# Rows of bounds for the gated-memory cells: by DMA through DRAM, or by TensorE and ScalarE

## What is computed

```python
b = jnp.cumsum(fc, axis=-1)
dlog = jnp.where(causal, b[..., :, None] - b[..., None, :] + ic[..., None, :], -jnp.inf)
inter = b + m[..., None]
m_t = jnp.maximum(inter, jnp.max(dlog, axis=-1))
w_in = jnp.exp(dlog - m_t[..., None])
s = jnp.einsum('bhtd,bhsd->bhts', qc, kc) * w_in
num = jnp.einsum('bhts,bhsd->bhtd', s, vc) + ...
den = jnp.sum(s, axis=-1) + ...
h = num / jnp.maximum(jnp.abs(den), jnp.exp(-m_t))[..., None]
```

## Time and profile before

| | us |
|---|---|
| runs of the kernel before | 3138.63, 3146.48, 3146.72 (median 3146.48) |
| the profiled execution's own time | 3142.69 |
| its span | 3140.9 |
| the cells stage, first spread to the end of the last product on DVE and the barrier | 1618.0 to 1735.4 |
| PE, DVE, ACT busy in 1618.0 to 1735.4 | 96.4, 78.3, 67.5 |
| DVE's first mask | 1624.77 |
| granted PE clock 0.50 (1.2 GHz) in the stage | 1639.4 to 1642.8, 1663.3 to 1666.7, 1711.2 to 1714.5, and from 1724.7 on |
| granted PE clock, mean of the whole | 0.978 |

### The profile page before, as it was taken

How to read it: one execution, slowest core, us unless ns; L and a number is a source line. 1 busy time by engine, 2 the same in 40 slices (tenths; PEclk the granted TensorE clock), 3 DMA queues, 4 the chain that set the end, 5 groups by cost and what they waited for, 6 DMA issues and landing times. The chain is left out here.

```text
span 3140.9 us, 37997 instructions
## 1 busy us (share of the span) xinstructions
PE 3025.9 (96%) x15290; PEld 2632.7 (84%) x15290; DVE 1923.5 (61%) x2891; ACT 1125.7 (36%) x1669; POOL 89.3 (3%) x72
## 2 busy tenths in 40 slices
PE   7989999999999999999998899999999999999998
PEld 5778888887788888899986499999999978788886
DVE  5755775856664878766646755543554365488674
ACT  4454422234453222343346123221222345343232
POOL 0031000000040000000000000000000000000000
PEclk9998999999998999999999899999999999999999
DMA  3110554521102655512110121121121210245432
GB/s 127 54 34 27 186 172 142 196 89 61 48 14 91 198 180 187 165 64 101 63 33 18 41 95 61 61 69 57 63 66 63 95 50 1 79 169 200 169 132 83
DMA packets 79546, 298.78 MB, mean 95 GB/s; under 512 B 8555, under 2 KB 12203, under 8 KB 78220
## 3 DMA queue, kind: packets, MB, share of 16 engines
q1 hardware_dynamic: 79372, 296.35, 28.0%
HBM read 287.93 MB, written 8.39 MB: 94 GB/s over the span
## 5 line engine op out<-in xcount | busy, mean ns | idle before, releaser
L122 PE MATMUL banks<-normed_hi,weights_hi 128*128 128x512 f32 (+2 forms) x2320 | 843.1, 363 | 0.8 <-DVE normed_lo L561 0.8
L123 PE MATMUL banks<-normed_lo,weights_hi 128*128 128x512 f32 (+2 forms) x2320 | 840.2, 362 | 0.0
L104 ACT ACTIVATE weights_hi<-weights_raw 128x1024 fp32r<-128x1024 f32 (+3 forms) x365 | 395.4, 1083 | 1221.4 <-PE banks L125 1178.3
L125 PE MATMUL banks<-normed_hi,weights_lo 128*128 128x512 f32 (+2 forms) x2320 | 737.8, 362 | 0.0
L110 DVE TENSOR_TENSOR weights_lo<-weights_raw,weights_hi 128x1024 fp32r<-128x1024 f32 (+3 forms) x365 | 463.0, 1269 | 145.4 <-ACT weights_hi L104 140.7
L123 PEld LDWEIGHTS banks<-normed_lo,weights_hi 128*128 128x128 f32 x2320 | 438.4, 189 | 41.2
L122 PEld LDWEIGHTS banks<-normed_hi,weights_hi 128*128 128x128 f32 x2320 | 437.0, 188 | 42.7 <-DVE normed_lo L561 1.2
L125 PEld LDWEIGHTS banks<-normed_hi,weights_lo 128*128 128x128 f32 x2320 | 429.6, 189 | 41.0
L122 PE MATMUL banks<-hidden_hi,weights_hi 128*128 128x512 f32 (+1 forms) x880 | 323.1, 367 | 0.1
L123 PE MATMUL banks<-hidden_lo,weights_hi 128*128 128x512 f32 (+1 forms) x880 | 323.0, 367 | 0.0
L125 PE MATMUL banks<-hidden_hi,weights_lo 128*128 128x512 f32 (+1 forms) x880 | 294.7, 367 | 0.0
(11 more groups left out here) (447 smaller groups left out, 4246.9 us busy)
## 6 DMA issues: line engine op xcount, KB each, us to landing
weights_raw<-in_w_up SPq DMA_DIRECT2D x176, 512.0 KB, 3.3
ada_tiles<-in_ada SPq DMA_DIRECT2D x96, 512.0 KB, 3.3
weights_raw<-in_w_down SPq DMA_DIRECT2D x64, 704.0 KB, 4.0
weights_raw<-in_w_in SPq DMA_DIRECT2D x67, 512.0 KB, 3.3
up_rows<-in_up_rows SPq DMA_DIRECT2D x44, 512.0 KB, 3.4
weights_raw<-in_w_out SPq DMA_DIRECT2D x32, 512.0 KB, 3.2
x_kept<-x SPq DMA_DIRECT2D x2, 3072.0 KB, 11.0
x<-x_kept SPq DMA_DIRECT2D x1, 3072.0 KB, 10.1
```

Source lines behind the costliest of these rows:

```text
L104: act.activation(self.hi[:, n % 2, 0:w], self.raw[:, n % 2, 0:w], ACT.Copy).then_inc(self.high_ready, 1)
L122: pe.matmul(out, self.hi[:, s, m], xh, start=k == 0, stop=False)
L123: pe.matmul(out, self.hi[:, s, m], xl, start=False, stop=False)
L125: mm = pe.matmul(out, self.lo[:, s, m], xh, start=False, stop=k == kt - 1)
```

## The change

The rows of bounds no longer go through PE, PSUM and ACT. SP stores M to a DRAM tensor once, when `gate_rows` is given, waits for it, and then loads one row of it to all 128 partitions for each run. The first two loads are issued before the last projection tile is evacuated. The others are issued one by one, when ACT and DVE are through with the buffer's last run. The buffers `bound_rows` now lie over M and the sums beside it, which are not read any more by then (hence the wait for `gate_cols`). DVE and ACT wait for the load of their run, each parity having its own semaphore. The spread on PE and the copies on ACT are gone, and with them the waits on them. The computation is the same.

```diff
+        self.bounds = Z.nc.dram_tensor("bounds", (64, TOK), F32).ap()
...
-        self.Mb = buf("bound_rows", [P, 2, TOK])
+        self.Mb = Z.buffer("bound_rows", [P, 2, TOK], 24 * TOK * ROW)
...
+    def bounds_in(self, n):
+        return self.Z.mix["bounds_odd" if n % 2 else "bounds_even"]
+
+    def bounds_there(self, eng, n):
+        eng.wait_ge(self.bounds_in(n), 16 * (n // 2 + 1))
+
     def sync(self, sp):
-        Z = self.Z
+        Z, on = self.Z, self.Z.mix
+
+        def spread(n):
+            h, d = self.RUNS[n]
+            if n >= 2:
+                sp.wait_ge(on["cell_decays"], 6 * (n - 1))
+                sp.wait_ge(on["cell_masked"], 6 * (n - 1))
+            sp.dma_start(self.Mb[:, n % 2], self.bounds[32 * d + h].partition_broadcast(P)).then_inc(self.bounds_in(n), 16)
+        sp.wait_ge(on["gate_rows"], 1)
+        sp.dma_start(self.bounds, self.gates.M).then_inc(on["bounds_kept"], 16)
+        sp.wait_ge(on["bounds_kept"], 16)
+        sp.wait_ge(on["gate_cols"], 1)
+        for n in range(2):
+            spread(n)
         sp.wait_ge(Z.evacuated, self.last + 1)
...
         sp.wait_ge(Z.mix["network_in"], 32)
+        for n in range(2, 8):
+            spread(n)
         sp.wait_ge(Z.mix["cell_scores"], 4 * self.PER_HEAD)
...
     def tensor(self, pe):
-        def spread(n):
-            h, d = self.RUNS[n]
-            if n:
-                pe.wait_ge(on["bounds_copied"], n)
-            else:
-                pe.wait_ge(on["gate_cols_copied"], 2)
-            sel = K["ident"][0:64, 32 * d + h:32 * d + h + 1].broadcast_to([64, P])
-            for seg, (a, w) in enumerate(SEGS):
-                mm = pe.matmul(Z.spread_ps[:, seg, 0:w], sel, self.gates.M[:, a:a + w], start=True, stop=True)
-            mm.then_inc(on["bounds_spread"], 1)
...
-                pe.wait_ge(on["bounds_copied"], 8)
+                pe.wait_ge(on["gate_cols_copied"], 2)
...
-        spread(0)
         pe.wait_ge(Z.evacuated, self.last + 1)
...
-                if m == 2 and n + 1 < 8:
-                    spread(n + 1)
                 pe.wait_ge(on["cell_weights"], 6 * n + m + 1)
...
     def scalar(self, act):
-        def copy_rows(n):
-            act.wait_ge(on["bounds_spread"], n + 1)
-            if n >= 2:
-                act.wait_ge(on["cell_weights"], 6 * (n - 1))
-            for seg, (a, w) in enumerate(SEGS):
-                last = act.activation(Mb[:, n % 2, a:a + w], Z.spread_ps[:, seg, 0:w], ACT.Copy)
-            last.then_inc(on["bounds_copied"], 1)
-            act.wait_ge(on["bounds_copied"], n + 1)
...
-        copy_rows(0)
...
+                if m == 0:
+                    self.bounds_there(act, n)
...
-                if m == 3 and n + 1 < 8:
-                    copy_rows(n + 1)
...
         def mask(q):
-            dve.wait_ge(on["bounds_copied"], n + 1)
+            self.bounds_there(dve, n)
```

More of the change, by code:

```diff
@@ L2494 @@
 class Cells(Stage):
-    COUNTS = ["v_cells_turned", "v_cells_copied", "bounds_spread", "bounds_copied", "cell_scores", "cell_scores_copied",
+    COUNTS = ["v_cells_turned", "v_cells_copied", "bounds_kept", "bounds_even", "bounds_odd", "cell_scores", "cell_scores_copied",
               "cell_masked", "cell_decays", "cell_weights", "cell_weights_used", "cells_out", "cells_step", "cell_squares",
```

## The result

| | before | after |
|---|---|---|
| median of 7 runs, us | 3143.88 (3138.63 to 3147.76) | 3124.08 (3121.37 to 3132.77) |
| ratio of times | | 0.9944, 95% interval 0.9929 to 0.9958 |
| profiled execution's own time | 3142.69 | 3132.77 |
| its span | 3140.9 | 3131.0 |

What follows compares the result with a forecast made beforehand. PE was taken to bound the kernel, busy 96% of the span; in the stage, PE bounds odd runs and DVE even ones. 4.47 + 2.61 + 2.93 + 0.25 = 10.26, minus 1.67, gives 8.6 us: 3134.1 us, range 3126.6 to 3143.

Steps and rivals of the forecast that it cites:

- The sum at full clock: Cells stage: gains of odd runs, even runs, first run and start add to 10.26 us at PE's full clock.
- odd runs 1, 3, 5: Direction 1 runs of the cells stage, bound by PE: each gains the spread's 1.49 us, 4.47 us together.
- even runs 2, 4, 6: Direction 0 runs, bound by DVE: each gains DVE's 0.87 us wait behind ACT's copy, 2.61 us together.
- run 0: First run of the cells stage: the late spread delays ACT's decays for step 4; removing it gains 2.93 us.
- start: First spread, ahead of the stage's first scores, which also need DVE's last evacuation: gain about 0.25 us.
- a fourth fall: Fifth or sixth run of the stage: a longer thin stretch of PE work brings another clock fall, costing 1.67 us.
- The transfers at nothing: SP's queue: all nine transfers cost 0 us, hidden by the run between; uncovered, each would cost 3.8 us.
- More than the sum: Rival, odd runs: DVE's whole waits go, 3 x 3.43 us, total 16.1 us, time 3126.6; chance 0.14.
- The clock gives it back: Rival: PE's clock falls four times, twice as long, returning 8.4 of 10.3 us, time 3140.8; chance 0.20.
- The rows come late: Rival: row loads landing in 13.7 us hold DVE's masks, six waits cost 27 us, time 3161; chance 0.06.
- The signs named: Expected in the new profile: third odd run at 11.1 us, even runs 9.4, decay waits some 12, four low stretches.
- The case of the three falls going: Cells stage: the three present clock falls disappear, put at -5.0 us as an end of the clock term.

Runs made afterwards that it cites:

- copies kept: Changed kernel with the two ACT copies of each run left at their old place, into an unread buffer, no spreads on PE: 3135.31 us, ratio 0.9971.
- spreads kept: Changed kernel with the two spread products of each run left on PE, their result unread, no copies on ACT: 3134.87 us, ratio 0.9968.
- moved: Changed kernel with DVE's hyena product and sum of squares, and ACT's squares, moved from even to odd runs: 3124.37 us, ratio 0.9949.
- Both kept: Changed kernel with spreads and copies left, waiting for each other as before, but the rows used come by DMA: 3142.81 us, ratio 1.0001.
- loads held back: Changed kernel with the later row loads asked for five steps later: 3139.37 us, ratio 0.9994.
- run 7: Not a follow-up: last of the cells stage's eight runs of six steps, odd, direction 1; with its tail 23.77 us in the kernel before.
- before_filled: Kernel before with unread PE products added, two in each even run and eight behind the last run: 3141.66 us, ratio 0.9991.

## Why the prediction was right or wrong

**The sum at full clock: right, and 1.1 us short.** The kernel before with its gaps filled and the changed kernel's second trace both have their runs at full clock (the falls in their tails cost 0.1 us at most), so their stages differ by the shortened path: 112.66 - 101.31 = 11.35 us, against 10.26.

| term | forecast | measured |
|---|---|---|
| odd runs 1, 3, 5 | 3 x 1.49 | 3 x 1.68 (12.61 - 10.93) |
| even runs 2, 4, 6 | 3 x 0.87 | 3 x 0.95 (10.29 - 9.34) |
| run 0 | 2.93 | 2.95 (10.73 - 7.78) |
| start | 0.25 | 0.44 (9.87 - 9.43) |

The odd runs gained what PE loses and not what DVE waited, as said: DVE had waited 3.44 us for the weights behind step 3, and at the same step of run 3, in the profile of after, it waits 1.04. Its wait got 2.40 us shorter and the run only 1.68.

```profile
1667.81 0.43 DVE L2778 TENSOR_TENSOR weights_st<-decays,scores 128x256 f32<-128x256 f32 x1 [1.04 <-ACT decays L2697]
```

The rest of the term is a size: the price of a spread is not only from its start to the next start. Before, the score product of step 2, the spread, and the products of step 2 kept PE for 0.95 + 1.49 + 0.99 = 3.43 us. Now PE's timeline of after has

```profile
1665.63 1.02 PE L2602 MATMUL banks<-qk 128*128 128x512 f32 x2
1666.49 1.05 PE L2642 MATMUL banks<-v_tokens,weights_st 128*128 128x129 f32 x8
1667.39 1.02 PE L2602 MATMUL banks<-qk 128*128 128x512 f32 x2
```

where score and products take 0.86 + 0.90 = 1.76. The difference is 1.67, so each neighbour of the spread had been longer by about 0.1. At the start, the spread kept alone costs 0.23 us, as the forecast had it, but the copy kept alone costs all of the 0.44; the forecast had not priced it. Run 0 shows the reverse: the copy alone costs it nothing and the spread alone 1.31 us. The 2.95 take both, with ACT waiting for PE's spread, which is the mechanism that the forecast named.

**The clock: the step that failed.** The forecast said "The change makes the thin stretch longer" and added 1.67 us for a fourth fall. It had the opposite sign. In the stage the falls had cost 4.6 us before (117.28 - 112.66), and the changed kernel paid 0.56 in its first trace (101.87 - 101.31) and nothing in its second. The hyena stretch is 1.5 us shorter too: it now meets a low stretch of 3.4 us, where before it began inside the one of 17.1. That is the rest of the gain: 11.35 + 4.62 + 1.5 = 17.5 us between the first trace of before and the second of after, where the ratios say 17.6 and 16.7. In place of 1.67 us lost to the clock, then, some 6.1 were won.

What the step left out is how PE's idle time lies. It compared PE's work with the length of the stretch, 3.48 us of 5.6 before and 1.93 of some 4.7 without the spread. But the copy on ACT also made a gap in it: it delayed step 4's decays, and so step 4's products on PE. PE's timeline of before in run 2 shows it (start, us, instruction, idle time before it):

```profile
1657.67 1.55 PE L2579 MATMUL banks<-bounds,consts 64*128 64x256 f32 x4
1659.23 1.31 PE L2634 MATMUL banks<-v_tokens,weights_st 128*128 128x129 f32 x6
1661.52 0.94 PE L2634 MATMUL banks<-v_tokens,weights_st 128*128 128x129 f32 x6 [0.97 <-DVE weights_st L2780]
1663.25 2.07 PE L2634 MATMUL banks<-v_tokens,weights_st 128*128 128x129 f32 x8 [0.80 <-DVE weights_st L2780]
```

and the changed kernel's, in its second trace, at the same steps:

```profile
1654.39 2.27 PE L2642 MATMUL banks<-v_tokens,weights_st 128*128 128x129 f32 x12 [1.49 <-DVE weights_st L2778]
1657.46 1.16 PE L2642 MATMUL banks<-v_tokens,weights_st 128*128 128x129 f32 x8 [0.80 <-DVE weights_st L2778]
```

Before, two gaps of 0.97 and 0.80 us have only 0.94 us of work between them, and the clock falls right behind, at 1663.3. Now the products of steps 2 to 4 go in one piece of 2.27 us between two gaps. With the copies kept, the gap at step 4 is back, and falls with it; with the spreads kept, the runs have neither. So the runs show that falls among them come with the copies, and the medians agree. That the copies do it by this gap was not tried by itself, and the gap cannot be the whole of it. Run 4 of before has it too, and no fall:

```profile
1686.09 0.94 PE L2634 MATMUL banks<-v_tokens,weights_st 128*128 128x129 f32 x6 [0.98 <-DVE weights_st L2780]
1687.82 1.16 PE L2634 MATMUL banks<-v_tokens,weights_st 128*128 128x129 f32 x8 [0.80 <-DVE weights_st L2780]
```

So does run 2 with the copies kept (0.92 and 0.80 us), and no fall comes there either. The first trace of after has a fall at the end of run 4, at 1677.6, without the gap, and the second has none. What decides between them stays open. The long fall at the stage's end has another tie: it is there with the spreads kept and not with the copies kept, but also in `moved`, which has neither. Why the change shortens it stays open too.

The Trainium skill's rule (TensorE: Matmul & The Clock Gate, part 1, "The HAM clock gate") is that PE is throttled unless activity releases it. The filler in the runs of the kernel before agrees, which won 4.6 us of the stage by adding work; the eight products at the stage's end, behind which the clock stood low for 10.2 us, do not show it. What I drew from the rule, that a kernel with less work on PE must fall more often, does not follow: 16 products fewer came with fewer falls.

**The transfers at nothing: right.** All landed in 3.3 to 4.7 us, and no engine waited for them. Both kept gives 1.0001, and only with the loads held back does a wait for them appear.

**The rivals.** "More than the sum" (3126.6) came nearest in time, but not by its mechanism: no odd run gained 3.43 us, and 11.35 us of the sum is all there is at full clock. Its time was right because the clock gave 6 us on top. "The clock gives it back" needed 8.4 us returned; it was the wrong sign. Its mechanism is real where only DVE's work is taken out: in `moved` three falls and the long one came back, though its odd runs grew more by PE work handed over than by the clock. "The rows come late" failed on its landing, 4.7 us at most where it needed 10.6.

**The signs named.** Odd run 5 took 11.47 us with the fall just ahead of it and 10.93 without, where 11.1 was named; even runs 9.34 (9.4); run 0 2.95 shorter (2.9); DVE's waits for decays 16.1 us (12). The four low stretches ahead of the one at the end did not come. The stretch behind the stage was not of the same length either, since the long low stretch had reached into it. The case of the three falls going stood in the text, at -5.0 us, but it got no rival of its own and no chance. With it the sum would have been 15.3 us and the time 3127.4, at the very edge of the range. What took the time past the edge is the 1.1 us by which the sum was short and the 1.5 us behind the stage, which no step had priced; they give 3124.8, and the rest, to 3124.1, is well within the spread of the seven runs.

## What to carry to other kernels

Moving a broadcast from PE and ACT to a DMA through memory pays by what it frees on the engine that binds each stretch: PE in one half of the runs, ACT's place in DVE's chain in the other. Price the clock in both directions whenever a change moves a wait on PE: not only how much PE works in a stretch, but where its gaps fall and what delays the work between them. Here the traces could say after the fact where falls came, but not foretell it, so such a term is better given as a range with both signs. And where a stage has cycles with different bounds, taking work out of the one that leaves PE waiting can cost as much in the next as it wins: partly because PE's last products move into the full run, and partly by the clock, which filling PE's gaps wins back.

## What was unexpected in the hardware

- Falls of the clock can come in the same places of a program from run to run: four in this stage in each of three traces of the old order, all at the same steps, 3.4, 3.4, 3.4 and 17.1 us long. In the changed kernel one of its falls came in one of two traces.
- A fall of 3.4 us costs 1.67 us where an odd run, full on PE, follows it, and 0.54 where it lies at the end of an even run, all of it paid in the next (run 5 of after: 11.47 against 10.93). In the tail of run 7 of the changed kernel it costs nothing measurable (22.43 and 22.45 us). In `before_filled`, without the fall at the turn of runs 6 to 7 and with the last low stretch reaching 2.8 us into the stage instead of 10.8, run 7 and its tail were 1.27 us shorter.
- One row of DRAM read for 128 partitions, 384 KB in SBUF, lands in 3.3 to 4.7 us, median 3.5, about as fast as the load of 512 KB of different data.
